# Sparse gather and add of expert rows by quarter rows, in a one-core decoder layer with a 32-expert mixture

## The chip, the cores and the metric

One NeuronCore of a Trainium2 chip runs the whole program. The metric is the time of one execution on the device in microseconds (us); the median of several executions is compared. The core has TensorE (PE: matmuls, with its weight loads as PEld), VectorE (DVE), ScalarE (ACT), GpSimd (POOL) and SyncE (SP), and 16 DMA engines that serve the queues of all of them. Engines run their own instruction streams in order and wait for each other by semaphores.

## The reference, cut to what matters

The layer mixes tokens (gated linear attention beside windowed attention), projects, normalises, and then sends each of 544 tokens to 4 of 32 experts. The change is about the last part; 544 x 4 / 32 = 68 rows per expert on average.

```python
x1 = layer_norm(DEEPNORM_ALPHA * x + mix, ln1_g, ln1_b)
logits = (xt @ w_router + b_router).astype(jnp.float32)
top_val, top_idx = lax.top_k(logits, TOP_K)
gate_w = jax.nn.softmax(top_val, axis=-1)
...
def expert_block(args):
    xe, e = args
    h = clamped_swiglu(xe @ w_gate[e] + b_gate[e], xe @ w_up[e] + b_up[e])
    return h @ w_down[e] + b_down[e]
...
out = jnp.zeros_like(xt).at[token_of].add(y_assign)
x2 = layer_norm(DEEPNORM_ALPHA * x1 + ffn, ln2_g, ln2_b)
```

All data are float32, D_MODEL is 1024, an expert has three matrices of 1024 x 1024 (4 MB each).

## The kernel before, in words

The program first computes the mixers and the first normalisation tile by tile (tiles 0 to 3 hold 128 prompt tokens each, tile 4 the 32 sample tokens), routes each tile, and writes the normalised rows x1 with their 32 gate weights behind them to a table in DRAM, `x1_dram` (x_rows in the trace). A second table, `acc_dram` (acc_rows), starts with the residual and collects the experts' results.

Then the experts go one after the other, each with up to 96 rows (CAP; further rows would go through an extra path that stays idle here). The weights stream through a ring of 16 slots of 1 MB (`ring_a`, `ring_b`, R2 = 16; 128 partitions of 8 KB each), four slots a matrix, twelve an expert (PER). SP issues each load as soon as its slot is free (`slot_used`), in the order up(e), gate(e+1), down(e).

One expert's rows on the way through the engines:
- DVE compares slot numbers with each token's place in the expert (`pick_rows`, writes `pick`), PE turns that into row numbers by five small matmuls (`rows_of`), DVE finishes them to integers (`read_rows`, writes `idx`).
- POOL gathers the rows of expert e+2 by one indirect DMA over 96 row numbers into `xg` (`gather`). A row is 4224 bytes: 1024 values and 32 gate weights.
- PE transposes `xg` in eight steps (`x_T`, L1243), ACT copies the result to `xeT` and the gate column to `gcol` (`rows_in`).
- PE runs the products (`product`, helper lines L1274 for gate and up, L1255 and L1258 for down), for which the 96 rows are split in three thirds j of 32 rows. PE's array is used in four column groups of 32. For gate and up, group q computes quarter q of the output columns for all thirds (`quarters`). For down (`tiles`), group j computes columns 0 to 767 of third j, and the fourth group the last 256 columns of all three.
- DVE and ACT apply biases, clamps and the sigmoid (`brow`, `gm`, `sg`, `hb`), and a 32 x 32 block transpose gives `heT` for the down product.
- ACT scales the result by the gate into `ysb` (`y_out`: one operation over 96 x 768, three copies through `yq`, one over 96 x 256), and POOL adds the rows to `acc_dram` by one accumulating indirect DMA (`add_rows`), waits for its landing, and counts `y_free`.

POOL's stream in a step e (`pool_step`) is: gather(e+2), then the add of expert e, then the wait for it. PE's stream (`pe_step`): x_T(e+1), rows_of(e+2), up(e), gate(e+1), down(e). Queues, loops over groups of four experts (TURN) and the order are all written by hand.

## Time and profile before

| | us |
|---|---|
| median of 3 runs | 1417.76 |
| lowest and highest | 1416.95, 1422.5 |
| the profiled execution | 1416.46 |
| its span on the core | 1414.6 |
| TensorE busy, share of the span | 96% |
| weights moved in the expert part | 384 loads of 1 MB |

The span runs from the first to the last instruction; the execution's own time is 1.9 us more. The part before the experts ends at about 336 us, the 32 experts end at 1382 us, and the second normalisation takes the rest.

### The profile page before, as it was taken

To read this page: it belongs to the slowest core of one execution; us is meant where nothing else is said; L and a number is where in the kernel's file an instruction comes from. 1 tells how busy PE (TensorE), PEld (TensorE's weight loads), DVE (VectorE), ACT (ScalarE), POOL (GpSimd) and SP (SyncE) were. 2 spreads that over 40 slices of the span, in tenths; PEclk is the share of its full clock that TensorE was granted. 3 is DMA by queue.
4 is the path that set the end of the run, shared out by engine and by line. 5 is a ranking of instruction groups with operands and counts; after the bars stand their busy time and mean duration, and the time that the engine had idled before them with its cause. 6 is when DMAs were issued, how large, how long until landed. Compare 5 with 4: busy or idle time off the path is not lost.

```text
span 1414.6 us, 43598 instructions
## 1 busy us (share of the span) xinstructions
PE 1358.3 (96%) x19522; PEld 872.2 (62%) x19522; DVE 440.2 (31%) x859; ACT 299.1 (21%) x637; POOL 120.4 (9%) x121
## 2 busy tenths in 40 slices
PE   7999999998999999999999999999999999999990
PEld 6767776555566666666666666666666666666660
DVE  3335656365322222222222222222222222222214
ACT  4544566131111111111111111111111111111104
POOL 1022000001010001000000100010000000100000
PEclk9999999998999999999999999999999999999995
DMA  8211042567999999999999999999999999999954
GB/s 276 60 50 46 16 145 74 210 234 280 413 405 397 405 401 405 397 403 403 406 403 403 403 403 396 403 401 407 397 404 401 408 401 401 401 399 389 405 216 135
DMA packets 78700, 459.80 MB, mean 325 GB/s; under 512 B 13344, under 2 KB 14896, under 8 KB 29232
## 3 DMA queue, kind: packets, MB, share of 16 engines
q1 hardware_dynamic: 67760, 429.74, 75.6%
q0 software_dynamic: 10256, 27.13, 7.2%
q8 instruction: 155, 2.54, 0.7%
q10 hardware_dynamic: 512, 0.26, 0.1%
q14 instruction: 17, 0.14, 0.0%
HBM read 443.85 MB, written 21.70 MB: 329 GB/s over the span
## 4 chain that ended last, share of the span: by engine, by line
PE 89%; DVE 6%; ACT 2%; issue 1%; DMA 1%; DVEq 0%; SPq 0%; ACTq 0%; POOLq 0%
PE unit L1274 47%; PE unit L1255 15%; PE unit L1258 9%; PE unit L1164 4%; PE unit L1243 3%; PE unit L763 2%; PE unit L765 2%; PE unit L764 2%; PE unit L758 1%; PE unit L891 1%; DVE attT L2185 1%; PE unit L915 1%; PE unit L798 1%; PE unit L1237 0%; ACT sbuf L1570 0%
## 5 line engine op out<-in xcount | busy, mean ns | idle before, releaser
L1274 PE MATMUL unit<-ring_b,xeT 128*32 128x256 f32 x6336 | 353.8, 381 | 1.1 <-ACT xeT L1420 1.1
L1274 PE MATMUL unit<-ring_a,xeT 128*32 128x256 f32 x5952 | 328.7, 379 | 0.0
L1274 PEld LDWEIGHTS unit<-ring_b,xeT 128*32 128x32 f32 x6336 | 203.7, 110 | 135.6 <-issue 2.7
L1274 PEld LDWEIGHTS unit<-ring_a,xeT 128*32 128x32 f32 x5952 | 192.6, 110 | 126.5
L1258 PE MATMUL unit<-ring_a,heT 128*32 128x256 f32 x768 | 169.7, 379 | 0.0
L1255 PE MATMUL unit<-ring_a,heT 128*32 128x512 f32 (+1 forms) x1536 | 169.4, 486 | 0.0
L1816 ACT ACTIVATE sg<-gm 128x768 f32<-128x768 f32 x32 | 27.0, 843 | 633.5 <-DVE gm L2456 633.5
L1258 PE MATMUL unit<-ring_b,heT 128*32 128x256 f32 x720 | 160.3, 379 | 0.0
L1255 PE MATMUL unit<-ring_b,heT 128*32 128x256 f32 (+1 forms) x1440 | 160.1, 486 | 0.0
L2484 DVE TENSOR_TENSOR hb<-unit,brow 128x768 f32<-128x768 f32 x32 | 30.7, 958 | 308.1 <-PE unit L1274 308.1
L700 POOL DMA_INDIRECT acc_rows<-ysb,idx x32 | 46.5, 1453 | 666.0 <-ACT ysb L1827 634.3
L1258 PEld LDWEIGHTS unit<-ring_a,heT 128*32 128x32 f32 x768 | 84.4, 110 | 27.1
L2454 DVE TENSOR_TENSOR gm<-unit,brow 128x768 f32<-128x768 f32 x32 | 30.7, 958 | 210.9 <-PE unit L1274 210.9
L1258 PEld LDWEIGHTS unit<-ring_b,heT 128*32 128x32 f32 x720 | 79.2, 110 | 25.4
L1823 ACT ACTIVATE ysb<-unit,gcol 96x768 f32<-96x768 f32 x32 | 28.7, 898 | 260.9 <-PE unit L1258 260.9
L1255 PEld LDWEIGHTS unit<-ring_a,heT 128*32 128x32 f32 x1536 | 63.1, 110 | 33.2 <-issue 0.8
L1255 PEld LDWEIGHTS unit<-ring_b,heT 128*32 128x32 f32 x1440 | 59.2, 110 | 33.3
L2370 DVE TENSOR_TENSOR row_part<-unit,ck 96x3 f32<-96x3 f32 x32 | 5.0, 156 | 224.1 <-PE unit L1237 224.1
L763 PE MATMUL unit<-hi_a,xth 128*128 128x512 f32 (+1 forms) x160 | 63.4, 396 | 3.9 <-DVE lo_a L1943 3.9
L667 POOL DMA_INDIRECT xg<-x_rows,idx x32 | 39.1, 1222 | 270.5 <-issue 267.8
L765 PE MATMUL unit<-hi_a,xtl 128*128 128x512 f32 (+1 forms) x160 | 60.4, 377 | 0.0
L764 PE MATMUL unit<-lo_a,xth 128*128 128x512 f32 (+1 forms) x160 | 60.2, 376 | 0.0
(318 smaller groups left out, 1264.8 us busy)
## 6 DMA issues: line engine op xcount, KB each, us to landing
ring_b<-w_gate_dram SPq DMA_DIRECT2D x68, 1024.0 KB
ring_a<-w_down_dram SPq DMA_DIRECT2D x68, 1024.0 KB
ring_b<-w_up_dram SPq DMA_DIRECT2D x64, 1024.0 KB
ring_a<-w_up_dram SPq DMA_DIRECT2D x64, 1024.0 KB
ring_a<-w_gate_dram SPq DMA_DIRECT2D x60, 1024.0 KB
ring_b<-w_down_dram SPq DMA_DIRECT2D x60, 1024.0 KB
raw_a<-w_in_dram SPq DMA_DIRECT2D x16, 512.0 KB, 3.7
wo<-w_out_dram SPq DMA_DIRECT2D x2, 1024.0 KB, 7.9
```

Source lines behind the costliest of these rows:

```text
L667: pool.indirect_dma_start(xg[:CAP], None, x1_dram, bass.IndirectOffsetOnAxis(ap=at, axis=0), bounds_check=T - 1, oob_is_err=False).then_in ...
L700: return pool.indirect_dma_start(acc_dram, bass.IndirectOffsetOnAxis(ap=at, axis=0), out, None, bounds_check=T - 1, oob_is_err=False, comp ...
L763: mm(out, xh, wh, start=start, stop=False)
L764: mm(out, xh, wl, start=False, stop=False)
L765: return mm(out, xl, wh, start=False, stop=stop)
L1164: ins = mm(bank(name)[:, h * HALF:(h + 1) * HALF], mix[i % 2][:, k], wo[:, k, h * HALF:(h + 1) * HALF], start=k == 0, stop=k == KD - 1)
L1243: ins = tr(px[:, k * P:k * P + CAP], half, ident[:CAP, :CAP])
L1255: return mm(out[j * NS:(j + 1) * NS, a:b], stat(j), w[:, a:b], start=first, stop=last)
L1258: return mm(out[CAP:P, j * 256:(j + 1) * 256], stat(j), w[:, FOLD:D], start=start, stop=stop)
L1274: ins = mm(dst, stat(j), own[:, q], start=first and j != 1, stop=last and j != 0)
L2454: tt(thirds(gm), thirds(pg), of_all(0), ALU.add).then_inc(h_part, 1)
L2484: tt(thirds(hb), thirds(pu), of_all(1), ALU.add).then_inc(h_part, 1)
```

## The change

x1 is written to DRAM so that a token has four rows of 288 values: quarter q of its columns (columns in the order that the block transpose needs) and behind it all 32 gate weights. For that POOL copies each tile in a permuted order (`x1_by_quarter`) before its DMA, and the gate weights are written four times. The row numbers are multiplied out over 128 partitions by one more small matmul (`to_quarters`) and a multiply and sum on DVE (`quarter_rows`): partition 32 q + s of column j holds the number of quarter q of slot 32 j + s. An expert's rows are then gathered by three indirect DMAs of 128 quarter rows (1152 bytes each), so that they lie in SBUF as the products need them but for 32 x 32 block transposes, which DVE does (`x_turned`, three of 128 x 256). PE's transposes and ACT's copy are gone. For experts 0 to 3 the three gathers are issued one behind the other; from the fifth expert on POOL waits for the landing of each before it issues the next.

The down product uses the same form as gate and up (`column_quarters`), so its result lies as 128 partitions x 3 thirds x 256 columns; ACT scales it in three operations, and POOL adds it by three accumulating indirect DMAs of 128 quarter rows (1024 bytes each), with one wait behind all three. `rows_of` and `pick_rows` work one expert further ahead. The samples' tile 4 is transposed and routed inside PE's product for tile 3 (out3) and on DVE ahead of tile 3's normalisation; before, it was routed behind it. Some constants and semaphores are merged; the extra path is adapted.

```diff
-        "out3", "x1T2", "x1T4", "logit2", "logit4", "x1T3", "logit3"]
+        "out3"]
+ROUTING = [("x1T4", 2), ("logit4", 1), ("x1T2", 3), ("logit2", 2), ("x1T3", 1), ("logit3", 3)]
...
+            def gather(n, par):
+
+                for j in range(3):
+                    if j and not (isinstance(n, int) and n < TURN):
+                        pool.wait_ge(x_rows, n * 48 + 16 * j)
+                        pool.sem_inc(turn_over, 1)
+                    pool.indirect_dma_start(xq[:, j], None, x1_quarters,
+                                            bass.IndirectOffsetOnAxis(ap=idxq[:, par % TURN, j:j + 1], axis=0),
+                                            bounds_check=4 * T - 1, oob_is_err=False).then_inc(x_rows, 16)
+
+            def x1_by_quarter(n, i):
+
+                r = rows(i)
+                if n >= 2:
+                    pool.wait_ge(x1_out, 16 * n)
+                ps(nc.gpsimd.tensor_copy(x1q[n % 2][:r].rearrange("p (q c b) -> p c q b", q=4, c=4),
+                                         res[:r, i].rearrange("p (c q b) -> p c q b", c=4, q=4)))
+                ps.settle()
+                pool.dma_start(x1_dram[i * P:i * P + r].rearrange("t (q f) -> t q f", q=4)[:, :, 0:QUARTER],
+                               x1q[n % 2][:r].rearrange("p (q f) -> p q f", q=4)).then_inc(x1_out, 16)
 
...
+            def add_quarters(par):
+
+                for j in range(3):
+                    pool.indirect_dma_start(acc_quarters, bass.IndirectOffsetOnAxis(ap=idxq[:, par, j:j + 1], axis=0),
+                                            ysq[:, j], None, bounds_check=4 * T - 1, oob_is_err=False,
+                                            compute_op=ALU.add).then_inc(y_stored, 16)
+
...
-                    pool.wait_ge(idx_ready, e + 3)
-                    pool.wait_ge(xT_done, e + 2)
+                    pool.wait_ge(idxq_ready, e + 3)
+                    pool.wait_ge(gcol_ready, e + 2)
                     pool.wait_ge(xe_ready, e + 2)
-                    pool.wait_ge(x_rows, (e + 2) * 16)
+                    pool.wait_ge(x_rows, (e + 2) * 48)
                     pool.sem_inc(turn_over, 1)
-                    gather(par + 2)
+                    gather(e + 2, par + 2)
...
-                add_rows(ysb[:CAP], idx[:CAP, par:par + 1]).then_inc(y_stored, 16)
-                pool.wait_ge(y_stored, e * 16 + 16)
+                add_quarters(par)
+                pool.wait_ge(y_stored, e * 48 + 48)
                 pool.sem_inc(y_free, 1)
...
+            def samples_routed(k):
+                if k == 4:
+                    x1_transposes(4)
+                if k == 5:
+                    logits(4)
+
+            out_product(3, samples_routed)
...
-            def x_T():
-                for k in range(KD):
-                    half = xg[:CAP, k // 2 * 256:(k // 2 + 1) * 256].rearrange("s (p k) -> s k p", k=2)[:, k % 2]
-                    ins = tr(px[:, k * P:k * P + CAP], half, ident[:CAP, :CAP])
-                ins.then_inc(xT_done, 1)
...
+            def to_quarters(n, out):
+
+                pe.wait_ge(idx_ready, n + 1)
+                mm(out, laneb[:CAP], spread[:CAP].rearrange("p j c -> p (j c)"), start=True, stop=True)\
+                    .then_inc(spread_done, 1)
...
+            def column_quarters(out, stat, w, first, last):
+
+                for j in range(3):
+                    for q in range(4):
+                        cols = slice(q * QUARTER, (q + 1) * QUARTER)
+                        ins = mm(out[q * NS:(q + 1) * NS, j * QUARTER:(j + 1) * QUARTER], stat(j), w[:, cols],
+                                 start=first and j != 1, stop=last and j != 0)
                 return ins
 
...
-                pe.wait_ge(x_rows, (e + 2) * 16)
-                pe.wait_ge(xe_ready, e + 1)
                 if e == 1:
                     pe.wait_ge(freed[3], USES[3] + 2)
-                x_T()
                 if not no_more:
-                    pe.wait_ge(picked, e + 3)
-                    pe.wait_ge(gate_read, e + 2)
-                    rows_of(tok_done, CAP)
+                    pe.wait_ge(idxq_ready, e + 2)
+                    to_quarters(e + 2, px[:, 0:9])
+                if e + 3 < NE:
+                    pe.wait_ge(picked, e + 4)
+                    pe.wait_ge(idx_ready, e + 3)
+                    rows_of(px, tok_done, CAP)
                 pe.wait_ge(h_ready, e + 1)
...
-                act.wait_ge(xT_done, n + 1)
...
-                copy(xeT[:, par], src).then_inc(xe_ready, 1)
+                act.wait_ge(x_rows, (n + 1) * 48)
+                src = xq[:, :, n + QUARTER:n + QUARTER + 1] if isinstance(n, int) else xq[:, :, bass.ds(n + QUARTER, 1)]
+                ins = copy(gcol[:, par:par + 1].rearrange("p a j -> p j a"), src)
...
-                act.wait_ge(xe_ready, e + 1)
-                nc.scalar.activation(ysb[:CAP, 0:FOLD], pd[:CAP, 0:FOLD], ACT.Identity, scale=gcol[:CAP, par:par + 1])
+                act.wait_ge(gcol_ready, e + 1)
                 for j in range(3):
-                    copy(yq[j * NS:(j + 1) * NS], pd[CAP:P, j * 256:(j + 1) * 256]).then_inc(y_part, 1)
-                act.wait_ge(y_part, e * 3 + 3)
-                nc.scalar.activation(ysb[:CAP, FOLD:D], yq[:], ACT.Identity, scale=gcol[:CAP, par:par + 1])\
-                    .then_inc(y_ready, 1)
+                    ins = nc.scalar.activation(ysq[:, j], pd[:, j * QUARTER:(j + 1) * QUARTER], ACT.Identity,
+                                               scale=gcol[:, par, j:j + 1])
+                ins.then_inc(y_ready, 1)
...
+            def quarter_rows(n, par, src):
+
+                v.wait_ge(spread_done, n + 1)
+                tt(row_parts[:, :, 0:3], src.rearrange("p (j c) -> p j c", j=3),
+                   k_("quarter").rearrange("p (j c) -> p j c", j=3)[:, :, 0:3], ALU.mult).then_inc(row_half, 1)
+                v.wait_ge(row_half, n + 1)
+                with nc.allow_low_precision(reason="row numbers: whole and small"):
+                    red(idxq[:, par], row_parts[:], ALU.add).then_inc(idxq_ready, 1)
+
+            def x_turned(n, par):
+
+                v.wait_ge(x_rows, (n + 1) * 48)
+                v.sem_inc(turn_over, 1)
+                for j in range(3):
+                    src = xq[:, j, 0:QUARTER].rearrange("p (c a k) -> p c k a", c=4, k=2)
+                    ins = nc.vector.transpose(xeT[:, par, j], src)
+                ins.then_inc(xe_ready, 1)
+
...
-                    read_rows(e + 2, (par + 2) % TURN)
-                    if not (isinstance(e, int) and e >= NE - 3):
-                        col = posm[:, :, e + 3:e + 4] if isinstance(e, int) else posm[:, :, bass.ds(e + 3, 1)]
-                        pick_rows(col, (par + 3) % ORDERS).then_inc(picked, 1)
+                    quarter_rows(e + 2, (par + 2) % TURN, px[:, 0:9])
...
+                if not (isinstance(e, int) and e >= NE - 3):
+                    read_rows(e + 3, px)
+                    if not (isinstance(e, int) and e >= NE - 4):
+                        col = posm[:, :, e + 4:e + 5] if isinstance(e, int) else posm[:, :, bass.ds(e + 4, 1)]
+                        pick_rows(col, par % ORDERS).then_inc(picked, 1)
...
+                if not no_more:
+                    x_turned(e + 2, par % 2)
```

POOL's stream in the loop over experts, one step, before (`DMA xg` is the gather, `DMA acc_rows` the add, the others are counters and branches):

```order
L707 REGISTER_ALU
L709 REGISTER_ALU
L667 DMA xg<-x_rows,idx 96x1056
L700 DMA acc_rows<-ysb,idx 544x1024
L719 ISA
```

The same step now:

```order
L756 REGISTER_ALU
L758 REGISTER_ALU
L693 DMA xg<-x_rows,idxq 128x288
L691 REGISTER_ALU
L693 DMA xg<-x_rows,idxq 128x288
L691 REGISTER_ALU
L693 DMA xg<-x_rows,idxq 128x288
L743 DMA acc_rows<-ysb,idxq 2176x256 x3
L768 ISA
```

One gather and one add became three and three, and at each L691 between the gathers stands the counter of a wait for the gather before.

PE's stream around the start of a step, before (the last rows of a down product, the transposes L1243, the row numbers L1237, the up and gate products L1274):

```order
L1258 MATMUL unit<-ring_a,heT 32x256
L1243 MATMUL unit<-ck,xg 128x96 x8
L1237 MATMUL unit<-tokb,pick 96x3 x5
L1274 MATMUL unit<-ring_a,xeT 32x256 x96
L1274 MATMUL unit<-ring_b,xeT 32x256 x96
L1255 MATMUL unit<-ring_b,heT 32x512 x3
```

And now (L1321 is the down product, L1313 up and gate):

```order
L1321 MATMUL unit<-ring_b,heT 32x256 x96
L1298 MATMUL unit<-spread,laneb 128x9
L1292 MATMUL unit<-tokb,pick 96x3 x5
L1313 MATMUL unit<-ring_b,xeT 32x256 x24
L1313 MATMUL unit<-ring_a,xeT 32x256 x48
L1313 MATMUL unit<-ring_b,xeT 32x256 x72
```

The eight transposes left the place between the down product and the next up product, and one small matmul came in; the down product's matmuls are all 256 columns wide.

DVE's stream at the end of a step, before (up to the gate product of the next expert; `brow` is the bias row):

```order
L2488 SCALAR_TENSOR_TENSOR gm<-hb,sg 128x768
L2446 REGISTER_ALU
L2448 STREAM_TRANSPOSE heT<-gm 128x768
L2434 ISA
L2436 STREAM_SHUFFLE brow<-brow 128x256
L2451 ISA
L2452 ISA
L2454 TENSOR_TENSOR gm<-unit,brow 128x768
```

And now:

```order
L2559 SCALAR_TENSOR_TENSOR gm<-hb,sg 128x768
L2517 STREAM_TRANSPOSE heT<-gm 128x768
L2427 TENSOR_TENSOR spread<-unit,ck 96x9
L2414 TENSOR_TENSOR pick<-ranks,posm 128x5x96
...
L2523 TENSOR_TENSOR gm<-unit,brow 128x768
L2524 REGISTER_ALU
L2525 TENSOR_SCALAR gm<-gm 128x768
L2529 TENSOR_TENSOR sg<-gm,sg 128x768
L2441 REGISTER_ALU
L2445 STREAM_TRANSPOSE xeT<-xg 128x256 x3
```

The first part of the row numbers and `pick` moved behind `heT`, and the step now ends with the transposes of `xg`, behind which DVE's next step stands.

## Rows read from the trace of the kernel before

**Rows 1.** The page: busy share of TensorE, and chain by engine.

```profile
PE 1358.3 (96%) x19522; PEld 872.2 (62%) x19522; DVE 440.2 (31%) x859; ACT 299.1 (21%) x637; POOL 120.4 (9%) x121
PEclk9999999998999999999999999999999999999995
PE 89%; DVE 6%; ACT 2%; issue 1%; DMA 1%; DVEq 0%; SPq 0%; ACTq 0%; POOLq 0%
```

**Rows 2.** Chain in order of time: start, length, what.

```profile
840.75 1.14 PE unit L1243 x8
842.07 20.86 PE unit L1274 x384
...
873.28 1.13 PE unit L1243 x8
874.60 20.86 PE unit L1274 x384
```

**Rows 3.** Timeline of TensorE between two experts: start, length, what.

```profile
808.14 1.20 PE L1243 MATMUL unit<-ck,xg 96*128 96x96 f32 x8
...
809.18 0.35 PE L1237 MATMUL unit<-tokb,pick 128*96 128x3 bf16 x5
...
809.46 10.57 PE L1274 MATMUL unit<-ring_a,xeT 128*32 128x256 f32 x192
```

**Rows 4.** Windows: busy time by engine, granted clock, DMA share, GB/s.

```profile
809.53:842.07 32.54, 32.54 (x545) 20.23 (x549) 7.77 (x14) 4.40 (x9) 2.57 (x2) 1.00 1.02 403
...
1355.00:1360.00 5.00, 5.00 (x100) 3.03 (x96) 0.00 (x0) 0.00 (x0) 0.00 (x0) 1.00 0.50 206
1360.00:1365.00 5.00, 5.00 (x82) 3.00 (x77) 3.46 (x4) 0.00 (x0) 0.00 (x0) 1.00 0.52 216
```

**Rows 5.** SP's issues of weight loads, early and late, and the last.

```profile
421.89 8.08 SPq L549 DMA_DIRECT2D ring_a<-w_gate_dram  x4
...
1310.82 2.65 SPq L549 DMA_DIRECT2D ring_b<-w_up_dram  x1
...
L549 SPq DMA_DIRECT2D ring_a<-w_down_dram x64: 327/333/5727, 370.3 to 1343.7; - x64
```

**Rows 6.** POOL's timeline over two steps, with idle time and releaser.

```profile
811.75 1.45 POOL L700 DMA_INDIRECT acc_rows<-ysb,idx  x1 [20.70 <-ACT ysb L1827]
821.46 1.12 POOL L667 DMA_INDIRECT xg<-x_rows,idx  x1 [8.26 <-issue]
844.29 1.46 POOL L700 DMA_INDIRECT acc_rows<-ysb,idx  x1 [21.70 <-ACT ysb L1827]
854.54 1.57 POOL L667 DMA_INDIRECT xg<-x_rows,idx  x1 [8.80 <-issue]
```

**Rows 7.** Groups of ACT and DVE, 419 to 1330: busy, mean ns.

```profile
L1420 ACT ACTIVATE yq<-unit 32x256 f32<-32x256 f32 x85 | 32.1, 378 | 1.7
L1823 ACT ACTIVATE ysb<-unit,gcol 96x768 f32<-96x768 f32 x28 | 25.1, 898 | 217.1 <-PE unit L1258 217.1
...
L1827 ACT ACTIVATE ysb<-yq,gcol 96x256 f32<-96x256 f32 x28 | 14.2, 508 | 0.9
...
L2448 DVE STREAM_TRANSPOSE heT<-gm 128x768 f32<-128x768 f32 x28 | 27.4, 978 | 1.0
```

**Rows 8.** DMA and POOL, 419 to 1330: queues; issue to landing; groups.

```profile
q1 hardware_dynamic: 47766, 347.85, 93.4%
q0 software_dynamic: 6272, 15.92, 7.2%
...
acc_rows<-ysb,idx POOLq DMA_INDIRECT x28, 9.0
xg<-x_rows,idx POOLq DMA_INDIRECT x28, 9.2
...
L667 POOL DMA_INDIRECT xg<-x_rows,idx x28 | 35.0, 1250 | 250.8 <-issue 250.8
```

**Rows 9.** Timelines ahead of the first expert: the first gather, SP's load behind it.

```profile
329.12 1.06 POOL L667 DMA_INDIRECT xg<-x_rows,idx  x1 [2.66 <-DVE idx L1914]
...
333.04 2.19 SPq L568 DMA_DIRECT2D ring_a<-w_down_dram  x4
```

**Rows 10.** Chain at the end: the last result, the last add.

```profile
1381.90 0.90 ACT ysb L1823
...
1385.38 4.99 DMA acc_rows<-ysb,idx
```

**Rows 11.** Windows and TensorE's timeline around the first product.

```profile
320.00:330.00 10.00, 6.26 (x48) 4.57 (x47) 8.05 (x34) 0.56 (x3) 2.49 (x4) 0.86 0.37 145
...
335.00:340.00 5.00, 3.95 (x39) 1.82 (x41) 2.70 (x3) 2.18 (x3) 2.13 (x3) 0.50 1.02 418
...
336.46 12.68 PE L1274 MATMUL unit<-ring_b,xeT 128*32 128x256 f32 x192 [1.05 <-ACT xeT L1420]
```

230 lines of the change are left out of this document (125 added, 105 removed).

## The prediction

> **What bounds the kernel now.** I read the page's shares and slices first, then the chain, then one expert in windows and timelines, then the DMA queues. TensorE is busy for 96% of the span at full clock, and the chain stands on it for 89% [rows 1]. The chain repeats with a period: the transposes (L1243) end one expert and the next two products begin 1.32 us after them, at 842.07 and 874.60, 32.53 us apart [rows 2]. Of those, 20.86 us are the up and gate products, about 10.35 the down product, 1.32 the work between: transposes from 808.14, the row-number product (L1237) at 809.18, next product at 809.46 [rows 2, 3]. TensorE is busy for all 32.54 us of such a stretch, so nothing else binds in it [rows 4].
>
> Two things stand close behind. First the weights: in the same stretch the 16 DMA engines have share 1.02 at 403 GB/s [rows 4]. Early on, four loads go out in 8.08 us with free slots setting the pace; late, one load alone takes 2.65 us to issue, so the queue has filled up: the stream falls slowly behind TensorE [rows 5]. The last weight load is issued at 1343.7, yet from 1355 to 1365 half of the share is still in use at about 210 GB/s: some engines are still 20 us and more behind while the others are done [rows 4, 5]. TensorE ends at 1381.9 and one load feeds 10.4 / 4 = 2.6 us of products, so if the weights alone set the end it would be near 1370 + 2.6, some 9 us earlier. A faster TensorE can gain no more than that.
>
> Second GpSimd: it starts an add at 811.75, the next gather at 821.46, the next add at 844.29. After each add it waits for the landing (9.7 and 10.25 us from start to next gather), and then it idles some 20 us until the next result [rows 6]. That idle time is the cover that this change spends.
>
> **The change, per expert.** TensorE loses the transposes and gains one tiny product: 1.32 becomes about 0.5 (the row-number rows last 0.35 us [rows 3]), so 0.8 is saved. The down product keeps its columns per group (3 x 256 a step instead of 512 + 256, and 3 x 256 in the fourth), and gate and up, which already have the new form, need 10.43 against 10.35: nothing. ScalarE loses the copy of xeT and its five result operations (898 + 3 x 378 + 508 = 2.5 us) become three of about 378, some 1.4 us less; VectorE gains three transposes, about 978 ns together by the row of the equal-sized heT [rows 7]. Both engines wait for TensorE most of the time: cost nothing while x arrives in time.
>
> **The DMAs.** In 28 experts the software queue moved 6272 packets, 224 each: 2 x 96 rows and 2 x 16 completions. So each row is a packet of its own, used or not [rows 8]. Now there are six DMAs of 128 rows: 6 x 144 = 864 packets. An engine gets 8 + 1 of each DMA in place of 6 + 1. The weight queue takes 93.4% of 16 x 911 us for 47766 packets, one in nine of them a completion: 0.285 us a packet, 0.32 a data packet [rows 8]. What a small packet costs beside full weight queues is seen in the latency: the first gather, with the weights at rest, is issued at 329.12 and the load that waits for it goes out by 333.04, 3.9 us; in the stream it takes 9.2. The last add lands in 5.0, in the stream 9.0 [rows 8 to 10]. No row shows the order of packets on an engine. I take it that each small packet of an engine waits for one weight packet. Then:
> - a gather of 8 + 1 packets instead of 6 + 1: 9.2 + 2 x 0.32 = 9.8 us;
> - three adds one behind the other, 27 packets instead of 7: 9.0 + 20 x 0.32 = 15.4, and 2 us more, because the third gather's packets stand ahead of them in the same queue: 17.4 us.
>
> The Trainium skill ("DMA: Bandwidth & Descriptors", Queues, rings and completion order) says that an engine goes round between its queues packet by packet, and that a packet usually holds 9 to 17 descriptors. The first half agrees with the latencies above; the second speaks for another sum (the second rival), and the 6272 packets of this trace disagree with it for rows of 4 KB.
>
> **Where the waits land.** From the fifth expert on GpSimd waits for gather 1 before it issues gather 2, and for 2 before 3. Behind these waits stand the adds of the expert before (the rows of POOL's order above), behind those y_free and the next expert's first gather. With the restart of 1.0 us after the adds (10.0 against 9.0), 0.2 us for a wait and 1.25 to issue the last gather [rows 6, 8], GpSimd's round is
> 17.4 + 1.0 + 2 x (9.8 + 0.2) + 1.25 + 0.3 = 39.9 us,
> above the 31.7 us that TensorE now needs. The 20 us of idle time are gone and 8 more. A second loop runs through TensorE: adds 17.4 + 1.0, three gathers 29.8, x transposed 1.2, gate and down products 20.9, results 1.2, all for two experts: 71.5 / 2 = 35.8.
>
> 39.9 is too much, because it assumes full weight queues. Engines need about 33.2 us an expert for what they carry now (at a period of 32.54 the late ones have fallen some 20 us behind after 30 experts: 32.54 + 20 / 30), and some 0.5 more for small packets (bounds 0 and 1.1: the software queue's 7.2% are 2.34 us an expert [rows 8], and quarter rows add nothing or half of it). Below 33.7 us the weights bind; above it the engines have idle time, in which small packets pass without waiting. At 36 this is 2.3 us, enough for up to some 20 of the 27 add packets at 0.1 us each, which saves up to 6 us; I take about half of it saved, 39.9 - 4 = 36, and the second loop agrees. I take 35.8.
>
> Bounds of the period: if the latency under load did not grow with packets, the adds would take 9.0 + 2 x 1.45 = 11.9, a gather 9.2, and the round 11.9 + 1.0 + 18.8 + 1.55 = 33.3, where the weights bind (33.7). If the idle time of the engines falls where it helps nothing, up to 38.
>
> **Start and end.** Routing the samples early puts 1.5 us of transposes and logits into out3's product, ahead of the last normalisation, and takes 3.3 us of VectorE's work out from behind it; but there the last tile's own transposes, logits and route set the time, so this is about 0. GpSimd's copies are before the last routing. The first expert needs three gathers: 2 x 1.06 us more to issue [rows 9], against 1.5 us less of transposes at half clock; with the index's way through TensorE, +2. Three experts at 0.8 us: -2. At the end three adds are issued instead of one, 2 x 1.45 and more packets, against 1.4 us less on ScalarE: +3.
>
> **Sum** against the profiled execution's 1416.46 us (1.3 below the median shown): 28 gathers with waits, 28 x (35.8 - 32.54) = +91; +2 - 2 + 3 = +3; so 1510 us, slower by 6.6%. Below 0.5% (7 us) I call it the same; that is about what a measurement of this kernel can tell.
>
> **Rivals.**
> 1. *GpSimd's round binds* (forecast), period 34.5 to 37.5: 1473 to 1558. For it: the measured latencies. Chance 0.70.
> 2. *The quarter rows share packets*, or small packets wait less than I think. If the eight rows of an engine went in one packet, a gather had 2 turns in place of 7, a round 10 + 1 + 2 x 8 + 1.5 = 28.5 us. Then only the weights bind: -9 (end) + 31 x 0.5 (small rows) + 3 = 1426; without sharing but at the bound of 33.7, 1416.5 + 28 x 1.16 + 3 = 1452. The page's packets of many descriptors would give this one. Against it: 96 packets for 96 rows, used or not. Chance 0.12, plus 0.06 that it comes out within 0.5% (small rows cost nothing, only the three extra microseconds are left).
> 3. *Faster*: the waits are covered and TensorE's 0.8 us counts 31 times, 25 us, of which the weight stream allows about 9: 1407. It decides if GpSimd's round stays below 31.7 us and small rows cost the slow engines under 0.3 us an expert. For it: 20 us of idle GpSimd. Against it: two landings in a row already take 18.4. Chance 0.06.
> 4. *The clock falls in every expert.* Ahead of the first expert TensorE is busy for only 6.26 of 10 us, and the granted clock falls to 0.50; the first product then takes 12.68 us where later ones take 10.43 [rows 11]. A stall of some 4 us an expert could do the same: 2 to 7 us lost each time. Part of it hides in the stall, as GpSimd's round does not need TensorE; if it does not, the period is 38 to 41: 1572 to 1656. Chance 0.06. The Trainium skill ("TensorE: Matmul & The Clock Gate", Part 1) has the idle array back at 1.2 GHz, which agrees with the 0.50.
>
> Range: 1425 to 1560 takes in cases 1 and most of 2; the likeliest one's own is 1473 to 1558. Slower 0.88, same 0.06, faster 0.06.
>
> **What would show it.** GpSimd's timeline: three gathers some 10 us apart, adds right behind them, no idle time but the landings, round 35 to 37 us from the fifth expert on, 32 before it. TensorE: one stall of 3 to 4 us an expert ahead of the gate product, released by VectorE's transpose of xg. DMA share below 1, under 380 GB/s. Packets of the software queue near 864 an expert. The prediction fails if a gather of quarter rows lands in 6 us or less, if the adds land together in under 10, or if the packets number far fewer.

## The result and the profile after

The changed kernel takes 1429.34 us (median of 5 runs, 1424.32 to 1433.54) against 1416.95 us (5 runs beside it): 1.008 times as long, 95% interval 1.0048 to 1.0112. So it is slower, as forecast, but by 12 us and not by 93; the time lies inside the range (1425 to 1560) and outside the range of the likeliest case (1473 to 1558). The profiled execution took 1427.94 us, its span 1426.1.

The page of the changed kernel: engines, queues, and the chain by engine and line.

```profile
PE 1350.0 (95%) x20830; PEld 940.0 (66%) x20830; DVE 468.8 (33%) x989; ACT 230.8 (16%) x541; POOL 294.6 (21%) x254
...
DMA 44%; PE 32%; issue 11%; DVE 5%; POOL 4%; ACT 2%; POOLq 1%; DVEq 0%; ACTq 0%; SPq 0%
DMA xg<-x_rows,idxq 23%; DMA acc_rows<-ysb,idxq 20%; PE unit L1313 11%; PE unit L1321 6%; PE unit L1213 4%; POOL acc_rows L743 3%; PE unit L812 2%; PE unit L814 2%; PE unit L813 2%; POOL xg L693 1%; PE unit L807 1%; PE unit L940 1%; DVE attT L2234 1%; PE unit L964 1%; PE unit L847 1%
```

TensorE is busy for 95% as before (96% in [rows 1]), and from this number alone nothing seems to have happened. The chain tells the rest: TensorE held 89% of it, now 32%, and the landings of gathers and adds hold 43%. The pace of the loop over experts is now set by GpSimd's round of DMAs.

That round, in GpSimd's timeline (start, length, what, idle time before it):

```profile
801.37 1.07 POOL L693 DMA_INDIRECT xg<-x_rows,idxq  x1 [10.93 <-issue]
809.02 1.03 POOL L693 DMA_INDIRECT xg<-x_rows,idxq  x1 [6.58 <-DMA xg<-x_rows,idxq]
816.63 1.00 POOL L693 DMA_INDIRECT xg<-x_rows,idxq  x1 [6.58 <-ACT ysb L1873]
818.20 1.63 POOL L743 DMA_INDIRECT acc_rows<-ysb,idxq  x1 [0.57 <-issue]
820.13 1.59 POOL L743 DMA_INDIRECT acc_rows<-ysb,idxq  x1 [0.30 <-issue]
822.02 1.57 POOL L743 DMA_INDIRECT acc_rows<-ysb,idxq  x1 [0.30 <-issue]
834.37 1.07 POOL L693 DMA_INDIRECT xg<-x_rows,idxq  x1 [10.77 <-issue]
```

Set it beside [rows 6]: the 20.7 and 21.7 us of idle time ahead of the add are gone. From first gather to first gather it is 33.0 us here, and 32.97 over 27 rounds (437.6 to 1327.8). It is made of 7.5 us from gather to gather, twice, 1.33 from the third gather to the first add, and 16.65 from the first add to the next gather (means over the loop): 32.98 by these rounded means.

The waits of this kernel from 419 to 1330 us (total, times, longest):

```profile
DVE xeT L2445 <- DMA xg<-x_rows,idxq: 451.4, 27, 20.7
...
POOL xg L693 <- DMA xg<-x_rows,idxq: 288.6, 45, 7.5
...
PEld unit L1313 <- DVE xeT L2445: 24.2, 14, 4.3
```

VectorE has no work for most of this wait; what counts is the last row, the x that comes too late for the gate product, in 14 of 28 experts and for 4.3 us at most. In TensorE's timeline one of them is this (start, length, what, idle time before it):

```profile
560.53 12.06 PE L1313 MATMUL unit<-ring_b,xeT 128*32 128x256 f32 x192 [2.71 <-DVE xeT L2445]
```

The DMA queues over the same stretch:

```profile
q1 hardware_dynamic: 47974, 349.34, 92.9%
q0 software_dynamic: 15984, 16.36, 8.2%
```

The software queue moves 571 packets an expert (15984 / 28), not the 864 of the prediction.

### The profile page after: what moved, and what is told of

Its sections match the earlier page's. It is cut to its first block, busy times and chain, and to the rows that moved or that the text cites. A ratio compares the mean times of both kernels' runs of the same rounds, so it can differ in the third digit from the quotient of the medians.

```text
span 1426.1 us, 46636 instructions
## 1 busy us (share of the span) xinstructions
PE 1350.0 (95%) x20830; PEld 940.0 (66%) x20830; DVE 468.8 (33%) x989; ACT 230.8 (16%) x541; POOL 294.6 (21%) x254
## 4 chain that ended last, share of the span: by engine, by line
DMA 44%; PE 32%; issue 11%; DVE 5%; POOL 4%; ACT 2%; POOLq 1%; DVEq 0%; ACTq 0%; SPq 0%
DMA xg<-x_rows,idxq 23%; DMA acc_rows<-ysb,idxq 20%; PE unit L1313 11%; PE unit L1321 6%; PE unit L1213 4%; POOL acc_rows L743 3%; PE unit L812 2%; PE unit L814 2%; PE unit L813 2%; POOL xg L693 1%; PE unit L807 1%; PE unit L940 1%; DVE attT L2234 1%; PE unit L964 1%; PE unit L847 1%
## 5 line engine op out<-in xcount | busy, mean ns | idle before, releaser
L1313 PE MATMUL unit<-ring_b,xeT 128*32 128x256 f32 x6336 | 370.3, 386 | 16.9 <-DVE xeT L2445 16.9
L1313 PE MATMUL unit<-ring_a,xeT 128*32 128x256 f32 x5952 | 338.9, 379 | 2.5 <-DVE xeT L2445 2.3
L1313 PEld LDWEIGHTS unit<-ring_b,xeT 128*32 128x32 f32 x6336 | 237.5, 111 | 131.9 <-DVE xeT L2445 22.0
L1313 PEld LDWEIGHTS unit<-ring_a,xeT 128*32 128x32 f32 x5952 | 232.9, 110 | 97.2 <-issue 5.1
L693 POOL DMA_INDIRECT xg<-x_rows,idxq x96 | 100.5, 1047 | 697.5 <-issue 363.3
L2445 DVE STREAM_TRANSPOSE xeT<-xg 128x256 f32<-128x256 f32 x96 | 35.2, 417 | 475.2 <-DMA xg<-x_rows,idxq 475.2
L1321 PE MATMUL unit<-ring_a,heT 128*32 128x256 f32 x3072 | 172.9, 379 | 0.0
L743 POOL DMA_INDIRECT acc_rows<-ysb,idxq x96 | 152.5, 1589 | 89.5 <-ACT ysb L1873 49.1
L1321 PE MATMUL unit<-ring_b,heT 128*32 128x256 f32 x2880 | 166.1, 379 | 0.2
L1321 PEld LDWEIGHTS unit<-ring_a,heT 128*32 128x32 f32 x3072 | 116.1, 110 | 51.5 <-issue 0.8
L1321 PEld LDWEIGHTS unit<-ring_b,heT 128*32 128x32 f32 x2880 | 116.0, 110 | 43.0 <-issue 1.3
L1873 ACT ACTIVATE ysb<-unit,gcol 128x256 f32<-128x256 f32 x96 | 38.5, 471 | 263.8 <-PE unit L1321 263.8
L2529 DVE TENSOR_TENSOR sg<-gm,sg 128x768 f32<-128x768 f32 x32 | 30.7, 959 | 28.4 <-ACT sg L1865 28.2
L812 PEld LDWEIGHTS unit<-hi_a,xth 128*128 128x128 f32 x160 | 31.2, 195 | 9.8 <-issue 4.9
L1990 DVE TENSOR_TENSOR lo_a<-raw_a,hi_a 128x1024 fp32r<-128x1024 f32 (+1 forms) x20 | 24.2, 1221 | 39.9 <-ACT hi_a L1472 39.0
```

Of the source, the lines that this page charges most:

```text
L693: pool.indirect_dma_start(xq[:, j], None, x1_quarters, bass.IndirectOffsetOnAxis(ap=idxq[:, par % TURN, j:j + 1], axis=0), bounds_check=4 ...
L743: pool.indirect_dma_start(acc_quarters, bass.IndirectOffsetOnAxis(ap=idxq[:, par, j:j + 1], axis=0), ysq[:, j], None, bounds_check=4 * T - ...
L812: mm(out, xh, wh, start=start, stop=False)
L1313: ins = mm(dst, stat(j), own[:, q], start=first and j != 1, stop=last and j != 0)
L1321: ins = mm(out[q * NS:(q + 1) * NS, j * QUARTER:(j + 1) * QUARTER], stat(j), w[:, cols], start=first and j != 1, stop=last and j != 0)
L1873: ins = nc.scalar.activation(ysq[:, j], pd[:, j * QUARTER:(j + 1) * QUARTER], ACT.Identity, scale=gcol[:, par, j:j + 1])
```

## The experiments

All times are medians, of 2 to 10 runs but for one kernel that ran once, as said there. The kernel before took 1417 to 1419 us beside them; ratios are to it, with 95% intervals.

**The round itself: no waits, a wait more, one wait.** The first run takes both waits between the gathers out.

```diff
-                    if j and not (isinstance(n, int) and n < TURN):
-                        pool.wait_ge(x_rows, n * 48 + 16 * j)
-                        pool.sem_inc(turn_over, 1)
                     pool.indirect_dma_start(xq[:, j], None, x1_quarters,
```

> The changed kernel without GpSimd's two waits between the three gathers of an expert; nothing else differs. Round theory (GpSimd's round of three gathers, adds and their landing is what takes 32.97 us an expert in the changed kernel): the three gathers go out about 1.3 us apart instead of 7.5, so the round needs 3 x 1.3 + 16.65 = about 21 us, falls below what TensorE and the weights need, and the period goes back to 31.9 to 32.6 us; time 1400 to 1420 us, not slower than the kernel before by over 0.5%. Rival (the small rows on the DMA engines cost the weight stream what was lost, wherever they are put): the period stays near 33.0 and the time near 1429. Second rival (the clock drops and stalls of TensorE come from late x for another reason): stalls ahead of the gate product stay.

1403.69 us, 0.990 (0.9879 to 0.9921): faster than the kernel before. The rival that has the small rows as the cause, wherever they are put, falls. TensorE's chain shows its own period, 31.56 us:

```profile
606.94 20.86 PE unit L1310 x384
627.80 10.36 PE unit L1318 x192
638.16 0.11 PE unit L1295
638.27 0.22 PE unit L1289 x5
638.50 20.86 PE unit L1310 x384
```

From about 970 us on it waits for weights now and then: the loads, 18 to 20 us from issue to landing between 450 and 550, take about 30 between 800 and 900. The mean over 27 rounds is 32.02.

The second run adds a wait for the third gather ahead of the adds.

```diff
                 pool.wait_ge(y_ready, e + 2)
                 pool.sem_inc(turn_over, 1)
+                if not isinstance(e, int) or TURN - 2 <= e < NE - 2:
+                    pool.wait_ge(x_rows, (e + 3) * 48)
+                    pool.sem_inc(turn_over, 1)
                 add_quarters(par)
```

> The changed kernel with one more wait of GpSimd per expert from the fifth on: for the third gather's landing, ahead of the three adds. Round theory: the third gather now costs 7.5 us like the first two instead of 1.3, but the adds no longer stand behind its packets, which may give 1 to 2 us back: the round goes from 33.0 to 37 to 39.5 us and the time to 1540 to 1610 us. Rival (the DMA engines' traffic sets the period, not the row of waits): no change, 1429.

1505.89 us, 1.061 (1.0573 to 1.0654), round 35.79 (435.4 to 1330.2, 25 rounds). The round theory holds in kind, but its ranges (37 to 39.5 us, 1540 to 1610 us) were too high. The queues are no longer full (q1 88.1% where the changed kernel has 92.9%), and the landing of the adds now varies; that fits the deduction in the prediction (idle time of the DMA engines lets small packets pass), but no run separates it from the other thing that changed, that the adds no longer stand behind the third gather's packets. From first add to next gather this kernel has 13.7 us on average, and its timeline 11.46 us and, one expert later, 16.57:

```profile
818.07 1.63 POOL L743 DMA_INDIRECT acc_rows<-ysb,idxq  x1 [6.13 <-DMA xg<-x_rows,idxq]
...
829.53 1.07 POOL L693 DMA_INDIRECT xg<-x_rows,idxq  x1 [6.09 <-issue]
...
850.83 1.63 POOL L743 DMA_INDIRECT acc_rows<-ysb,idxq  x1 [6.95 <-issue]
...
867.40 1.07 POOL L693 DMA_INDIRECT xg<-x_rows,idxq  x1 [11.18 <-issue]
```

The third has one wait (`if j == 2 and ...`): two gathers together, the third when both have landed.

> The changed kernel with only one of the two waits: the first two gathers of an expert back to back, the third when both have landed. Round theory: 33.0 - 7.5 + 1.3 = 26.8 us and a little more for two gathers landing together, below TensorE's 31.4; so the weights and TensorE bind as without waits: 1400 to 1408. Rival (two gathers back to back are enough to stall TensorE's instructions in each expert): 1415 to 1430.

1407.85 us, 0.9915 (0.9898 to 0.9932); the round is 31.91. As expected.

The last of these puts a wait for the gather into the kernel before, ahead of its add.

```diff
+                if not isinstance(e, int) or e < NE - 2:
+                    pool.wait_ge(x_rows, (e + 3) * 16)
+                    pool.sem_inc(turn_over, 1)
```

> The kernel before with one more wait of GpSimd per expert: for the landing of its one gather, ahead of the add. Cover theory (GpSimd idles some 20 us there, so a wait of 9 us costs nothing, and what made the changed kernel slow is that two waits of 7.5 us and a longer add no longer fit into the period): no change, 1413 to 1421 us. Rival (a wait behind a gather costs by itself, wherever it stands, by what its semaphore and restart take on GpSimd): 28 x 1 us or more, 1445 and up.

1420.24 us, ratio 1.0005 (0.999 to 1.0019). A wait under cover costs nothing here: it stands in every expert, behind a landing of some 9 us [rows 8], and no time is lost.

**What sets the landings.** The adds become plain scatters (`compute_op=ALU.add` taken out): the rows are written, and the sum over a token's experts is left out.

> The changed kernel with its three adds as plain scatters: the rows are written and not summed (the sum over a token's experts is left out). Theory that an accumulating row of 1 KB is always a packet of its own and a plain one shares: packets of the software queue fall from 571 an expert to below 400, first add to next gather falls from 16.65 us to about 10, the round from 33.0 to about 26.5, and the weights or TensorE bind at 31.9 to 32.6: time 1400 to 1420. Rival (sharing depends on the direction, not on the summing, and the time is the way to memory and back): packets and the 16.65 us stay, time 1429.

1390.87 us, 0.980 (0.9776 to 0.9829), faster than the 1400 to 1420 expected: GpSimd's round no longer binds, and the period is TensorE's own, 31.58. Its queues:

```profile
q1 hardware_dynamic: 49652, 361.04, 95.3%
q0 software_dynamic: 8208, 16.95, 4.9%
```

Half of the software packets are gone with the same bytes. The counts can be taken apart. The row-add kernel below has 29 adds of 96 rows (96 + 16 packets each) and 84 gathers in 7280 packets: (7280 - 29 x 112) / 84 = 48 per gather, 16 completions and 32 for 128 rows, so four rows share a packet. The sizes in the changed kernel's packet records say the same slot by slot: 4608, 3460, 2312 and 1164 bytes are four, three, two and one used rows of 1152 bytes, with 4 bytes for each unused slot. The changed kernel's 84 adds are then (15984 - 84 x 48) / 84 = 142, 128 + 16 within 2%: each accumulating row of 1 KB is a packet of its own. Plain ones share (8208 less 84 x 48, over 87, is 48 again). First add to next gather falls from 16.65 us to 10.6 as expected. Of these 6 us 1.8 may be GpSimd's own: plain scatters are issued every 1.31 us, accumulating ones every 1.91.

Then the weight loads of experts 5 to 28, cut to half of each partition's bytes and to 64 bytes.

```diff
-                    sp.dma_start(ring[m % R2], w).then_inc(w_in2[m % R2], 16)
+                    if it is None:
+                        sp.dma_start(ring[m % R2], w).then_inc(w_in2[m % R2], 16)
+                    else:
+                        sp.dma_start(ring[m % R2][:, 0:1], w[:, 0:1]).then_inc(w_in2[m % R2], 16)
```

> The changed kernel whose weight loads in the loop (experts 5 to 28) bring only the first of the two rows of each partition, 4 KB instead of 8 KB a packet (the products then use stale values for the other half: part of the computation is left out). Theory of the prediction (each small packet of an engine waits behind one weight packet): the weight queue is idle half the time and its packets are half as long, so a gather falls from 7.5 us to 4 to 5, first add to next gather from 16.65 to 10 to 12, the round from 33.0 to 20 to 24 and TensorE binds at about 31.7: time 1400 to 1412. Rival (gathers and adds have a fixed latency of their own in the chip, whatever the weights do): 7.5 and 16.65 stay, time 1429.

> The changed kernel whose weight loads in the loop bring only 64 bytes a partition (the products use stale values for the rest: part of the computation is left out), so that gathers and adds go over nearly idle DMA engines. Linear theory (a landing is a fixed part plus a wait behind weight packets, in proportion to their length): with 8 KB packets a gather is 7.5 us from start to start, with 4 KB 5.7, so with none it is 3.9; the adds with their landing are 16.65, 10.6 to 11, and so 5 to 6 here. Rival (half the weights already leave the engines idle time, so nothing more is gained): 5.7 and 10.6 stay. In both TensorE binds: 1390 to 1396 us.

1395.6 us with half the weights (below the 1400 to 1412 expected) and 1396.68 us with nearly none (a single run, just above its 1390 to 1396). With half of them gather to gather is 5.8 us on average from 480 to 1200 us (expected 4 to 5: missed) and the adds' stretch 10.5. With nearly none, GpSimd's timeline reads:

```profile
806.74 1.63 POOL L746 DMA_INDIRECT acc_rows<-ysb,idxq  x1 [14.71 <-issue]
...
816.49 1.66 POOL L696 DMA_INDIRECT xg<-x_rows,idxq  x1 [4.36 <-issue]
820.90 1.03 POOL L696 DMA_INDIRECT xg<-x_rows,idxq  x1 [2.75 <-DMA xg<-x_rows,idxq]
824.62 1.00 POOL L696 DMA_INDIRECT xg<-x_rows,idxq  x1 [2.69 <-DMA xg<-x_rows,idxq]
```

Gather to gather is 4.4 and 3.7 us here, with a median of 3.9 in the same stretch (expected 3.9); the adds' stretch is 9.75, and 8.75 an expert later, 9.1 on average (expected 5 to 6: missed). So a quarter-row gather is some 3.9 us of its own and 3.6 of waiting behind weight packets. With half the weights half of that wait is left; but these loads have shorter packets and also leave the engines idle time (q1 60.9% from 480 to 1200 us, 92.8% in the changed kernel), and no run parts the two. The adds are 9 of their own and 7.5 behind full queues; most of that goes with half the weights (10.5), so their wait isn't in proportion.

**One part alone: quarter gathers, but the down product, ScalarE's results and the add in whole rows as before.** The core of the edit (row numbers of whole rows come from `idxq`):

```diff
-                add_quarters(par)
-                pool.wait_ge(y_stored, e * 48 + 48)
+                add_rows(ysb[:CAP], idx[:CAP, par:par + 1]).then_inc(y_stored, 16)
+                pool.wait_ge(y_stored, e * 16 + 16)
...
-                    product(pd, h_of(heT), m0 + 8, range(4), column_quarters)
+                    product(pd, h_of(heT), m0 + 8, range(4), tiles)
```

First without the waits between the gathers.

> The changed kernel without the two waits and with the down product, ScalarE's results and the add as the kernel before has them (one add of 96 whole rows), so that of the change the quarter-row gathers, VectorE's transposes and the early routing are left. To be set against 1403.69 us, the same with adds in quarters. Theory (the small accumulating packets take weight stream time: 273 packets of 1 KB at 0.101 us are 1.72 us an engine and expert, 68 rows of 4 KB at 0.327 are 1.39; plain adds, which share packets, brought the time to 1391): 0.33 us an expert comes back, minus 10 us at most: 1393 to 1399. Rival (the down product's form and ScalarE's shorter results are what brings e1's gain): slower, 1410 to 1417. Second rival (both forms of the add cost the stream the same): 1402 to 1405.

1432.55 us, 1.0099 (1.008 to 1.0118): all three readings missed. GpSimd idles 19 us an expert and neither x nor weights are late, yet TensorE needs 33 us. Where it loses them is told below. Then with the waits of the changed kernel.

> The changed kernel with its two waits, but with the down product, ScalarE's results and the add in whole rows as in the kernel before. Round theory: one add and its landing take 10.2 us (rows of before), two waits 2 x 7.5, the third gather's issue 1.3, in all 26.5 us, below the 31.4 that TensorE needs: GpSimd's idle time covers the waits, and since the gathers are apart, the stalls of TensorE of the row adds without waits (1432.55 us) are gone: 1396 to 1408. Rival (row adds themselves stall TensorE or the weights): 1425 to 1433.

1395.06 us, 0.983 (0.9809 to 0.985), 1 us below the range expected. GpSimd's timeline:

```profile
803.49 1.49 POOL L751 DMA_INDIRECT acc_rows<-ysb,idx  x1 [6.43 <-ACT ysb L1897]
813.57 1.04 POOL L695 DMA_INDIRECT xg<-x_rows,idxq  x1 [8.59 <-issue]
820.40 1.00 POOL L695 DMA_INDIRECT xg<-x_rows,idxq  x1 [5.79 <-DMA xg<-x_rows,idxq]
827.35 1.00 POOL L695 DMA_INDIRECT xg<-x_rows,idxq  x1 [5.95 <-issue]
835.04 1.49 POOL L751 DMA_INDIRECT acc_rows<-ysb,idx  x1 [6.69 <-ACT ysb L1897]
```

It waits 6.4 to 6.7 us for ScalarE's result: the same two waits fit, because one add and its landing take 10.1 us here (10.6 on average) where three take 16.65. TensorE's chain is 31.55 us an expert up to 1273 us.

**TensorE's loads with gaps.** What the waits are good for shows where they are missing. The first sign was the late routing: the kernel without waits, with the samples routed where the kernel before has them (the lines of `ROUTING`, `samples_routed` and the order on ScalarE and VectorE undone).

> The changed kernel without the two waits and with the samples routed where the kernel before routes them (after the last x1). It is to be set against the same without the waits and with early routing, 1403.69 us. Theory of the prediction (early routing is about nothing: the last tile's own transposes, logits and route set the time of the first gather): 1402 to 1405. Rival (early routing took the last normalisation 2.6 us back and gave back less): faster by 1 to 3 us, 1400 to 1402. Second rival (it saves what it takes out from behind the last normalisation, 1.5 us of TensorE and 3.3 us of VectorE): slower, 1406 to 1408.

1428.26 us, 1.0062 (1.0043 to 1.008), 25 us more than with early routing, which none of the three readings allows. Its weight loads have gaps (TensorE's loads, timeline):

```profile
806.35 0.33 PEld L1321 LDWEIGHTS unit<-ring_b,heT 128*32 128x32 f32 x4
806.94 0.16 PEld L1321 LDWEIGHTS unit<-ring_b,heT 128*32 128x32 f32 x5 [0.26 <-issue]
807.69 0.18 PEld L1321 LDWEIGHTS unit<-ring_b,heT 128*32 128x32 f32 x5 [0.59 <-issue]
808.45 4.24 PEld L1321 LDWEIGHTS unit<-ring_b,heT 128*32 128x32 f32 x81 [0.58 <-issue]
```

and beside them, in GpSimd's timeline of the same kernel:

```profile
804.13 1.07 POOL L690 DMA_INDIRECT xg<-x_rows,idxq  x1 [11.09 <-issue]
805.51 1.04 POOL L690 DMA_INDIRECT xg<-x_rows,idxq  x1 [0.31 <-issue]
806.85 1.00 POOL L690 DMA_INDIRECT xg<-x_rows,idxq  x1 [0.30 <-issue]
```

Five loads, a gap of 0.59 us with nothing to wait for, five loads again, beside the third gather. This is so in every expert of this kernel and of the row adds without waits, there in the middle of the gate product, since the gathers come earlier. In the changed kernel such a row of gaps stands only beside two triples without waits, at 371 and 410 us (the third and fourth expert's gathers). But it has single, shorter gaps too: 21 of 0.15 to 0.50 us in the loop, most of them 1.5 us after the first add goes out, which is where a gather and two adds are issued back to back. The first add of this one is at 519.00:

```profile
520.52 2.58 PEld L1313 LDWEIGHTS unit<-ring_b,xeT 128*32 128x32 f32 x52 [0.44 <-issue]
```

They cost little while GpSimd's round binds. But the no-wait kernel above (1403.69) has such triples all along and not these gaps (three single ones of over 0.5 us, after 1040 us). It differs from the late routing in the order of the routing, so the next runs change only where TensorE's instructions lie: two more small products ahead of the second logits (`keep_running("logit2", 4)`), and then no product at all:

```diff
             keep_running("logit2", 2)
+            for _ in range(8):
+                pe.sem_inc(turn_over, 1)
             logits(2)
```

> The changed kernel without the two waits, and with two more of TensorE's small products ahead of the second logits (they compute nothing that is used), some 1 us before the experts, behind which all of TensorE's later instructions lie a little further on. Seen so far: with three gathers back to back TensorE stood still for 1 to 1.7 us in each expert, in gaps of 0.59 us after every five weight loads, within 1 us of the third gather (late routing 1428.26 us, row adds 1432.55), but not in the kernel without the waits and early routing (1403.69). Placement theory (whether the stall comes is set by where TensorE's instructions lie): the stalls appear in each expert and the time goes to 1425 to 1435. Rival (it is set by something else, the order of the routing or the row adds): no stalls, 1401 to 1407.

> The changed kernel without the two waits, and with eight semaphore increments of TensorE's queue ahead of the second logits: they compute nothing and take no time on the array, but all later instructions of TensorE lie eight instructions further on. Placement theory: the stalls of TensorE's instructions beside the back-to-back gathers come back in each expert, as with two more small products (1424.28 us): 1418 to 1430. If no stalls come (1401 to 1407), then either eight instructions are another favourable distance, or the small products' time and not their place did it; the placement theory is then weaker.

1424.28 us, 1.0032 (1.0015 to 1.0048), and 1423.35 us, 1.0035 (1.002 to 1.0051). Eight increments that run once, some 20 us ahead of the first product, cost 20 us against 1403.69. TensorE's wait row of the last one, and below it that of the kernel without waits:

```profile
PEld unit L1320 <- issue: 35.1, 73, 0.6
```

```profile
PEld unit L1318 <- issue: 3.0, 5, 1.3
```

35.1 / 28 = 1.25 us an expert, and the rounds are 32.70 us against the 31.56 of TensorE alone. The kernel without waits has 32.02 on average, since weights hold it up late; 27 rounds of the difference, 0.68, are 18 of the 20 us. So the place of TensorE's instructions matters, as expected. But the theory as I put it has a hole: the changed kernel has TensorE's instructions of the no-wait kernel to the last one, and it has gaps at 371 and 410 us, where the no-wait kernel has none. So three more shifts of the no-wait kernel: eight increments on GpSimd's queue ahead of its first gather, one on TensorE's in place of eight, eight on ScalarE's.

> The changed kernel without the two waits (1403.69 us, no stalls of TensorE's instructions), with eight semaphore increments on GpSimd's queue ahead of its first gather; TensorE's instructions are the very same. The placement theory as it was stated (the place of TensorE's instructions decides): 1401 to 1407, no stalls. Against it: the changed kernel itself has the same TensorE instructions too, and stalls at the two triples without waits near 371 and 410 us, where the kernel without waits has none. Rival (the place of GpSimd's instructions, or how the two lie to each other, decides as well): stalls in each expert, 1418 to 1430.

> The same kernel with one increment on TensorE's queue in place of eight (1423.35 us with eight). If any shift of TensorE's instructions brings the stalls, 1418 to 1430; if it takes a certain distance, 1401 to 1407.

> The same kernel with eight increments on ScalarE's queue, ahead of its last exponential before the experts; TensorE's and GpSimd's instructions are the very same. If the lie of all engines' instructions decides, stalls and 1418 to 1430; if only TensorE's and GpSimd's count, 1401 to 1407.

1406.66, 1406.11 and 1402.84 us, 0.9903 (0.9862 to 0.9944), 0.9919 (0.989 to 0.9948) and 0.9896 (0.9867 to 0.9925), and no such rows of gaps. So it takes more than one instruction's shift on TensorE, and a shift of GpSimd's or ScalarE's start alone doesn't do it. The hole stays: what the waits in GpSimd's loop change for the triples ahead of them is open, and so is what at the place decides.

The late routing with the waits, in both forms of the add, then prices early routing.

> The changed kernel with its two waits and with the samples routed where the kernel before routes them. Theory (GpSimd's round sets the period, early routing is about nothing, and the waits keep the gathers apart, so that no stalls of TensorE's instructions come from them): 1427 to 1432, no stalls but those ahead of the gate product. Rival (late routing is what slows TensorE, not the back-to-back gathers): stalls of 1 to 1.7 us stay in each expert; where they fall before the x rows are late they cost nothing, so the time stays about the same, and the trace tells.

> The row adds with waits (1395.06 us), with the samples routed where the kernel before routes them. Here TensorE alone sets the period, so the start shows in the end. Theory of the prediction (early routing is about nothing): 1393 to 1397. Rival (it made the last normalisation 2.6 us later): 1392 to 1393. Second rival (it saves the work behind the last normalisation): 1397 to 1399.

1431.99 us, 1.0083 (1.0058 to 1.0108), against 1429.34 for the changed kernel; and 1392.94 us, 0.9817 (0.9795 to 0.9839), against 1395.06. One difference has each sign and the intervals overlap: early routing is worth nothing that can be measured. The rows of gaps are gone in both but at the first triples, which have no waits; with quarter adds single ones of 0.15 to 0.43 us are left beside the adds, as in the changed kernel. That also settles the late routing's 25 us: it was not the routing's own work.

Last, the row adds with the waits from the third expert on (`n < 2` in place of `n < TURN`).

> The row adds with waits (1395.06 us), with the two waits already between the gathers of the third and fourth expert, where one stall of TensorE's instructions (1.5 us) was left in the third. Theory (every back-to-back triple costs what it stalls): 1 to 2 us faster, 1393 to 1394. Rival (two landings more, at the start, when GpSimd is still behind, make the third or fourth expert's x late): 1396 to 1402.

1396.27 us, 0.9824 (0.9798 to 0.9851), against 1395.06: not told apart by five runs each. The trace has no gaps left, and it has what the rival said, one x that is late by more than the gaps were worth:

```profile
435.15 13.39 PE L1315 MATMUL unit<-ring_b,xeT 128*32 128x256 f32 x192 [3.41 <-DVE xeT L2472]
```

## Why the prediction was right in sign and wrong in size

- **What binds.** Right: GpSimd's round took TensorE's place in the chain, the 20 us of idle time went, the adds stand right behind the third gather. One wait less or both gone give 1407.85 and 1403.69 us, one more 1505.89. What failed are terms of the sum; the first below is the largest.
- **The step that failed: "I take it that each small packet of an engine waits for one weight packet. Then: a gather of 8 + 1 packets instead of 6 + 1: 9.2 + 2 x 0.32 = 9.8 us".** A gather and its wait take 7.5 us, not 9.8 + 0.2. That gathers wait behind weight packets holds (3.9 us with nearly no weights, 5.8 with half, 7.5 with all). The count was wrong: quarter rows of a gather share packets, two data packets an engine in place of eight. The prediction carried the count of 4 KB rows [rows 8] over to 1 KB rows, and kept what the second rival says for another sum. With the right count its own rule gives 9.2 - 4 x 0.32 = 7.9 us. This is 2 x 2.5 = 5.0 us of the round. The price of one turn is not shown by this: three packets an engine at 0.32 are 1.0 us, and the wait measured is 3.6.
- **"and 2 us more, because the third gather's packets stand ahead of them in the same queue: 17.4 us"** is mis-sized by those 2 us. First add to next gather was to be 18.4 us and is 16.65; without waits, where the gathers have long landed, it is 16.84. The rest of this sum comes out, 10.43 in the kernel before plus 20 x 0.32 is 16.8, and the accumulating rows are indeed 128 + 16 packets an add. But part of that is luck. An add and restart at rest are 5.0 [rows 10] and some 1.0, and three quarter adds with nearly no weights take 9.1: by this estimate about 3 of the 6.4 us come from issuing and landing three adds, with no weight packet to wait for.
- **"39.9 - 4 = 36, and the second loop agrees".** The undiminished sum with the measured terms is 2 x 7.5 + 1.33 + 16.65 = 32.98, the round measured; nothing is to be deducted, for at 33 us the queues are as full as before (92.9% against 93.4%). So two errors stood against each other, 6.9 us too much in the sum and 4 taken off it, and 2.8 were left (35.8 against 32.97): 28 x 2.8 = 78 of the 81 us by which the forecast of 1510 was too high. Adds that land faster show only where the round is longer, with the third wait, at 35.79 us. That the forecast has 35.8 too is chance: that kernel has one more wait.
- **"Below 33.7 us the weights bind" and TensorE's gain.** Wrong: the kernel without waits carries the same small packets and ran at 32.02 us an expert over 27 rounds, at 31.56 up to about 970 us, where the loads begin to come late. The row adds with waits kept 31.55 for most of the loop. TensorE's need of 31.7 was right within 0.15. The estimate from how late the slow engines were (32.54 + 20 / 30) gave a need that these kernels stay below; why those engines were late is not shown.
- **The second rival** named the cause that failed the forecast, sharing of packets, and gave 1426 us, near the result of 1429.34. That nearness is chance: it had the round at 28.5 us and the weights binding, while in truth the round binds, because sharing came for the gathers and not for the adds. The Trainium skill ("DMA: Bandwidth & Descriptors", Queues, rings and completion order) has a typical packet hold about 9 to 17 descriptors; here the packets held four rows for 1152-byte gathers and one for accumulating rows.
- **Start and end.** The first gather went out at 330.64 (329.12 in [rows 9]) and the first product began at 338.46, 2.0 us later than before: as forecast. The tail is 33.6 us from TensorE's end to the end of the span against 32.7: +0.9, forecast +3. Early routing 0, as forecast.
- **The clock.** The granted clock fell to 0.50 behind four stalls of TensorE, of 2.2 to 3.8 us, and not in each expert; the product at 560.53 above is one, 12.06 us where others take 10.57. The fourth rival did not come.
- **The sum.** 27 rounds of 32.97 - 32.54 us are +11.6 us; with the start's 2 and the tail's 0.9 that is 14.5. The profiled executions differ by 11.5 us (1427.94 and 1416.46). The 3 us between them fit three experts without waits, 1 us quicker each (32.54 - 31.56; forecast 0.8).

So of the change the quarter gathers and VectorE's transposes are worth 1.7%. The quarter adds, with the down product's and ScalarE's new form, give it all back under the waits: 34 us between 1395.06 and 1429.34. That it is the adding and not the form is shown by the plain scatters, which keep the form and take 1390.87. The waits bind only together with these adds: they cost 26 us against the kernel without them (1403.69), and 5 to 6 against the two in which TensorE's loads also have gaps (1424.28 and 1423.35).

## What to carry to other kernels

Before spending an engine's idle time on waits, write its round as a sum of latencies, and take the packet count of a DMA from a DMA of the same row size and kind: gathered, plain and accumulating rows are packed differently. When two parts are changed together (gathers and adds), cost and measure each alone; the fastest complete kernels here, at 1393 to 1396 us, have the gathers and not the adds. When an edit that only moves instructions changes the time by over 1%, look for idle time of TensorE's loads with nothing to wait for, beside software DMAs issued back to back, before explaining the time by the edit.

## What the runs showed of the hardware

- Beside three indirect gathers issued 1.36 us apart TensorE's loads stood still for 1.2 us, in gaps of about 0.59 us between five weight loads (four kernels), or not at all (four others, that differ by a few instructions). With 7 us between the gathers and row adds it did not happen; with two together or with quarter adds right behind the third there were single gaps of 0.15 to 0.5 us in about half to three quarters of the experts. Instructions come over DMA queues too: in the kernel without waits the queue `instruction` moved 130 packets and 2.13 MB from 419 to 1330 us. The Trainium skill ("Runtime: NRT & Kernel Launch", Instruction fetch mechanics) says that instructions are refilled in blocks of 16 KiB, which agrees with these packets, and that the cost is mostly hidden. That the gaps are this cost coming to light, by late refills of TensorE's instructions, is a guess: no run here shows it.
- Gathered rows of 1152 bytes share packets, four slots in each. Accumulating rows of 1 KB do not, and plain ones of 1 KB do: 48 packets for 128 rows against 144. Plain scatters took the software queue's share from 8.2% to 4.9%. A row of 4224 bytes was a packet of its own.
- Issuing an accumulating scatter of 128 rows keeps GpSimd for 1.91 us, a plain one for 1.31.
